# A pair's first product copied into the bank of its second summand, and T4 in place of B22, in a block chain of fp32 layers on one core

## The chip, the core and the metric

The kernel runs on one core of a Trainium2 chip. The metric is the device time of one execution in microseconds (us), median of several runs. A NeuronCore has five engines with a queue of instructions each: PE (TensorE, matrix products), ACT (ScalarE), DVE (VectorE), POOL (GpSimd) and SP (SyncE, which here only issues transfers). They run side by side and wait for each other by semaphores only. Sixteen DMA engines carry out what SP, POOL and ACT issue. TensorE reads SBUF and writes PSUM, which has 8 banks of 128 x 512 fp32.

## The reference

The input is 256 tokens of 1024 features. The program is a chain: a convolution module, an FFN, a gated injection (PLE), a differential attention block, a second FFN, a second PLE, and a second block with ten input projections. What the change touches are the two FFNs, with d_ff = 2816:

```
def swiglu(x, w_gate, w_up, w_down):
    return (jax.nn.silu(x @ w_gate) * (x @ w_up)) @ w_down
...
u = rms_norm(h, ffn_norm_g[i])
h = h + swiglu(u, ffn_w_gate[i], ffn_w_up[i], ffn_w_down[i])
```

## The kernel before

**Pieces.** All weights are cut into pieces of 128 x 2048 fp32 (1 MB). Each piece is an operation o in one fixed order (STREAM, FFN_ORDER, lines 54 to 72). SP loads pieces in that order into a ring of four buffers (`raw`, line 337); a buffer is free when the low part of its old piece has been made. For precision each piece is split in two: ScalarE rounds it to `w_hi` (high part, line 1191), VectorE subtracts to get `w_lo` (low part, line 1737). Both have three slots, so ScalarE runs at most three pieces ahead of PE. `ahead(o)` makes the parts up to piece o+2. PE multiplies high by high, low by high, high by low.

**FFN.** The 11 chunks of 256 hidden columns (gate and up, 512 output columns) go by STEPS: chunks 0, 1 and 10 alone (`single`), and the pairs (2,3), (4,5), (6,7), (8,9) by `pair`. A pair is a 2x2 block product: two token tiles, two halves of the contraction, two chunks. It takes seven products instead of eight, by Strassen's method in Winograd's form. The left sums are made once in a layer by POOL (`first_sums`: `q_f32`, then `q_hi` by ScalarE at line 1278 and `q_lo` by POOL at 1106). The right sums are T1 = B11+B12, T2 = T1+B22 (VectorE, line 1853), T3 = T2+B21, T4 = B12+B22; they live in the three slots of `sums`: T1 in 0, T2 and then T3 in 1, T4 in 2. T1, T3 and T4 are made by POOL's transfers, one that loads and one that adds into SBUF while it moves (`accum_op`; T3 only adds to T2). T4's two transfers are issued a pair ahead, when the old T4's low part is made (lines 1127 to 1129). B22 is loaded twice, once into the ring for its own product and once inside T4.

**Order of a pair on PE** (line 578): B11, transposes of a finished chunk, T1, T2, transposes, B22, down piece, B21, T4, down piece, T3. Banks before: B11, then T2, T4 and T3 in b1; T1, then B22 in b4; B21 in bank 2; b1 and b4 change places from pair to pair. Bank 3 holds transposes, banks 4 to 7 the down product's sums.

**Order on ScalarE** (line 1286), a strict queue: high part o+2; silu of the last quarter of the pair before; copy of the first product to c_11 (1295); high part o+3 (B22); z_hi (1247); copy c_22 (1299); high part o+4; z_hi; copy c_12 (1304); high parts o+5 and o+6 (T4); silu of a quarter; o+7, o+8; two silus (1255); o+9, o+10.

**Order on VectorE** (line 1877): low part o+2; gate of the last quarter of the pair before (1838); z_lo (1831); low parts o+3, o+4; z_lo; c_12 (1892); o+5; a gate; o+6, o+7; c_11 (1900); c_22 (1903); a gate; o+8; a gate; o+9; T2 of the next pair; o+10.

POOL's order in between is `first_sums` and `weight_sums` (lines 1090 to 1130). Before these, in layer 0, POOL issues the write `toep` to DRAM at line 1055 and later two loads from it.

Of the kernel before, what the change touches and what calls it, by code (L numbers as in the profile page):

```python
# [31 lines left out]
RAW, SPLIT = 4, 3  # L32
# [52 lines left out]
SUM_SLOT = {"T1": 0, "T2": 1, "T3": 1, "T4": 2}  # L85
# [36 lines left out]
def build(nc, ws, x_tok, p_feat, par, rows, lam_rows, rel, onehot, sgu_w, pool_m, toep, u_scr, out):  # L122
    ctx = ExitStack()
    with ctx:
# [68 lines left out]
        c_11, c_22, c_12 = view(2048, 512), view(2560, 512), view(3072, 512)  # L193
# [79 lines left out]
        def operand(o):  # L273

            if o in SUM_OF_OP:
                return sums[:, SUM_SLOT[SUM_OF_OP[o][2]], :]
            return raw[:, PIECE_OF[o] % RAW, :]

        def loaded(eng, p):

            eng.wait_ge(raw_loaded[p % RAW], 16 * (p // RAW + 1))

        def operand_there(eng, o):

            if o in SUM_OF_OP:
                layer, p, name = SUM_OF_OP[o]
                sum_there(eng, layer, p, name)
            else:
                loaded(eng, PIECE_OF[o])

        def sum_there(eng, layer, p, name):

            n = pair_no(layer, p)
            if name == "T1":
                eng.wait_ge(S("t1_in"), 32 * n)
            elif name == "T4":
                eng.wait_ge(S("t4_in"), 32 * n)
# [19 lines left out]
        def _(sp):  # L317
# [5 lines left out]
            for g in range(1, NPIECE):  # L323
# [13 lines left out]
                sp.dma_start(raw[:, g % RAW, :], ws[g]).then_inc(raw_loaded[g % RAW], 16)  # L337
# [14 lines left out]
        def _(pe):  # L352
# [167 lines left out]
            def ffn(layer, m):  # L520
# [44 lines left out]
                def single(i):  # L565

                    token_chunk(("gu", layer, i), ffn_at(layer, "gu", i, 0), x_hi, x_lo,
                                ready=ready_from(m) if i == 0 else None, at={0: (0, 1), 1: (0, 2), GU - 1: (1, 2)}[i],
# [9 lines left out]
                def pair(p):  # L578
# [16 lines left out]
                    product(("p2", n), ffn_at(layer, p, "B21"), *of_x(1, t0), b2, True, (S("c_11"), 2 * n))  # L595
# [378 lines left out]
        def _(pool):  # L974
# [66 lines left out]

            def biased(n_):
# [36 lines left out]
            def second_part(name, layer, p):  # L1079

                n = pair_no(layer, p)
                if name == "T1":
                    pool.wait_ge(S("t1_in"), 32 * n - 16)
                    pool.dma_start(sums[:, 0, :], ws[B12_ROW[layer, p]], accum_op=ALU.add).then_inc(S("t1_in"), 16)
                else:
                    pool.wait_ge(S("t4_in"), 32 * n - 16)
                    pool.dma_start(sums[:, 2, :], ws[PIECE_OF[ffn_at(layer, p, "B22")]], accum_op=ALU.add) \
                        .then_inc(S("t4_in"), 16)

            def first_sums(m):  # L1090

                layer, p = PAIRED.index(m), PAIRS[0]
                pool.dma_start(sums[:, 0, :], ws[PIECE_OF[ffn_at(layer, p, "B11")]]).then_inc(S("t1_in"), 16)
# [16 lines left out]
                pool.dma_start(sums[:, 2, :], ws[B12_ROW[layer, p]]).then_inc(S("t4_in"), 16)  # L1110
                second_part("T4", layer, p)
# [7 lines left out]
            def weight_sums(layer):  # L1119

                for before, p in zip(PAIRS, PAIRS[1:]):
                    lo_ready(pool, ffn_at(layer, before, "T1"))
                    sum_there(pool, layer, before, "T2")
                    pool.dma_start(sums[:, 0, :], ws[PIECE_OF[ffn_at(layer, p, "B11")]]).then_inc(S("t1_in"), 16)
                    third_sum(layer, before)
                    second_part("T1", layer, p)
                    lo_ready(pool, ffn_at(layer, before, "T4"))
                    pool.dma_start(sums[:, 2, :], ws[B12_ROW[layer, p]]).then_inc(S("t4_in"), 16)
                    second_part("T4", layer, p)
                third_sum(layer, PAIRS[-1])  # L1130
# [12 lines left out]
            for n_ in range(2):  # L1143
# [3 lines left out]
                pool.tensor_tensor(st2[:, c], st2[:, c], st2[:, 56:57].to_broadcast([P, 8]), ALU.pow).then_inc(S("o_r"), 1)  # L1147
            pool.wait_ge(S("h_done"), 16)
# [32 lines left out]
        def _(act):  # L1181
# [59 lines left out]
            def ffn(layer, m, gname):  # L1241
# [44 lines left out]
                def pair(p):  # L1286
# [8 lines left out]
                    act.activation(c_11, bank[:, :], ACT.Copy).then_inc(S("c_11"), 1)  # L1295
# [15 lines left out]
                    act.wait_ge(S("c_11"), 2 * n)  # L1311
                    gated(one, 0, c_11[:, 0:256])
# [407 lines left out]
        def _(dve):  # L1720
# [102 lines left out]
            def ffn(layer, m, gname):  # L1823
# [19 lines left out]
                def second_sum(p):  # L1843
# [7 lines left out]
                    g = PIECE_OF[ffn_at(layer, p, "B22")]  # L1851
                    loaded(dve, g)
# [667 lines left out]
```

## Time and profile before

| | us |
|---|---|
| median of 3 runs (lowest, highest) | 1044.75 (1043.84, 1048.94) |
| the profiled execution's own time | 1044.09 |
| its span in the trace | 1042.3 |
| PE busy | 1004.0 |
| VectorE busy | 726.8 |
| ScalarE busy | 579.1 |
| first products of the pairs of layer 0, start | 132.56 |
| first products of the pairs of layer 1, start | 470.19 |

The span is shorter than the execution's time by 1.8 us, which lie before the first and behind the last instruction of the trace. The profile's weights and sums carry the name `arena` where they lie in the big scratch tensor (`sums` does), `raw` where they are in the ring. Busy time of matmuls is modelled at their ends. In rows in order of time, the brackets give the idle time before an instruction and what ended it.

### The profile page before, as it was taken

To read this page: it belongs to the slowest core of one execution; us is meant where nothing else is said; L and a number is where in the kernel's file an instruction comes from. 1 tells how busy PE (TensorE), PEld (TensorE's weight loads), DVE (VectorE), ACT (ScalarE), POOL (GpSimd) and SP (SyncE) were. 2 spreads that over 40 slices of the span, in tenths; PEclk is the share of its full clock that TensorE was granted. 3 is DMA by queue.
4 is the path that set the end of the run, shared out by engine and by line. 5 is a ranking of instruction groups with operands and counts; after the bars stand their busy time and mean duration, and the time that the engine had idled before them with its cause. 6 is when DMAs were issued, how large, how long until landed. Compare 5 with 4: busy or idle time off the path is not lost.

```text
span 1042.3 us, 13575 instructions
## 1 busy us (share of the span) xinstructions
PE 1004.0 (96%) x5398; PEld 846.7 (81%) x5398; DVE 726.8 (70%) x866; ACT 579.1 (56%) x697; POOL 168.4 (16%) x140
## 2 busy tenths in 40 slices
PE   9999959999999999998999999999999999999997
PEld 8967847877888888786778788788888888999886
DVE  6986649778757776767888766776454557777554
ACT  6427536666556677655666647654545454344433
POOL 4982530010020310171110002100000000000000
PEclk9999989999999999999999999999999999999999
DMA  8866889999554533579999854556555445554531
GB/s 322 267 189 119 308 223 319 318 302 333 216 173 150 202 133 110 187 262 258 341 331 328 253 203 160 217 194 230 186 189 202 155 169 191 177 199 162 202 121 41
DMA packets 35422, 225.23 MB, mean 216 GB/s; under 512 B 4248, under 2 KB 6808, under 8 KB 9504
## 3 DMA queue, kind: packets, MB, share of 16 engines
q1 hardware_dynamic: 24480, 171.45, 44.5%
q0 software_dynamic: 7856, 49.73, 19.1%
q10 hardware_dynamic: 3024, 3.18, 1.2%
q8 instruction: 43, 0.70, 0.3%
q14 instruction: 19, 0.16, 0.0%
HBM read 221.14 MB, written 3.21 MB: 215 GB/s over the span
## 4 chain that ended last, share of the span: by engine, by line
PE 77%; DVE 7%; DMA 5%; issue 5%; POOL 4%; ACT 1%; POOLq 0%; DVEq 0%; ACTq 0%
PE bank L393 48%; PE bank L515 10%; PE bank L484 4%; DVE w_lo L1737 4%; DMA toep<-bias_row 3%; PE bank L381 3%; PE bank L379 3%; PE bank L380 3%; DMA arena<-in_ws 2%; PE bank L429 2%; DVE arena L1853 2%; DVE arena L1838 1%; POOL w_lo L1010 1%; POOL arena L1102 1%; POOL arena L1101 1%
## 5 line engine op out<-in xcount | busy, mean ns | idle before, releaser
L1737 DVE TENSOR_TENSOR w_lo<-raw,w_hi 128x2048 fp32r<-128x2048 f32 x149 | 346.1, 2326 | 151.6 <-ACT w_hi L1191 151.1
L1191 ACT ACTIVATE w_hi<-raw 128x2048 fp32r<-128x2048 f32 x160 | 305.8, 1913 | 135.1 <-PE bank L393 115.9
L393 PE MATMUL bank<-w_hi,x_hi 128*128 128x512 f32 x544 | 149.5, 397 | 0.2
L393 PE MATMUL bank<-w_lo,x_hi 128*128 128x512 f32 x544 | 145.7, 390 | 0.0
L393 PE MATMUL bank<-w_hi,x_lo 128*128 128x512 f32 x544 | 145.7, 389 | 0.0
L393 PEld LDWEIGHTS bank<-w_hi,x_lo 128*128 128x128 f32 x544 | 102.1, 188 | 21.8
L393 PEld LDWEIGHTS bank<-w_lo,x_hi 128*128 128x128 f32 x544 | 102.1, 188 | 21.4
L393 PEld LDWEIGHTS bank<-w_hi,x_hi 128*128 128x128 f32 x544 | 98.9, 188 | 21.1 <-issue 1.8
L393 PE MATMUL bank<-w_hi,z_hi 128*128 128x512 f32 x320 | 94.2, 394 | 0.1
L393 PE MATMUL bank<-w_lo,z_hi 128*128 128x512 f32 x320 | 93.0, 390 | 0.2
L393 PE MATMUL bank<-w_hi,z_lo 128*128 128x512 f32 x320 | 92.8, 390 | 0.0
L1191 ACT ACTIVATE w_hi<-arena 128x2048 fp32r<-128x2048 f32 x32 | 61.6, 1926 | 54.9 <-DMA arena<-in_ws 19.8
L1737 DVE TENSOR_TENSOR w_lo<-arena,w_hi 128x2048 fp32r<-128x2048 f32 x32 | 72.6, 2284 | 20.0 <-ACT w_hi L1191 20.0
L381 PE MATMUL bank<-x_hi,w_lo 128*128 128x256 f32 x256 | 72.4, 283 | 0.0
L380 PE MATMUL bank<-x_lo,w_hi 128*128 128x256 f32 x256 | 72.4, 283 | 0.0
L379 PE MATMUL bank<-x_hi,w_hi 128*128 128x256 f32 x256 | 72.4, 283 | 0.0
L393 PEld LDWEIGHTS bank<-w_lo,z_hi 128*128 128x128 f32 x320 | 59.9, 188 | 13.5 <-DVE w_lo L1737 1.0
L393 PEld LDWEIGHTS bank<-w_hi,z_lo 128*128 128x128 f32 x320 | 60.1, 188 | 12.7
L1010 POOL TENSOR_TENSOR w_lo<-raw,w_hi 128x2048 fp32r<-128x2048 f32 x11 | 50.7, 4615 | 115.8 <-ACT w_hi L1191 105.3
L393 PEld LDWEIGHTS bank<-w_hi,z_hi 128*128 128x128 f32 x320 | 58.9, 188 | 12.0 <-issue 0.6
L1173 POOL TENSOR_SCALAR st<-st 128x1 f32<-128x1 f32 x2 | 0.5, 225 | 301.8 <-ACT arena L1232 301.8
L379 PEld LDWEIGHTS bank<-x_hi,w_hi 128*128 128x128 f32 x256 | 49.1, 192 | 0.0
(282 smaller groups left out, 1475.7 us busy)
## 6 DMA issues: line engine op xcount, KB each, us to landing
raw<-in_ws SPq DMA_DIRECT2D x160, 1024.0 KB, 4.9
arena<-in_ws POOLq DMA_DIRECT2D x40, 1024.0 KB, 10.8
arena<-u_scr ACTq DMA_DIRECT2D x16, 142.0 KB, 4.8
arena<-in_rows POOLq DMA_DIRECT2D x2, 1024.0 KB, 5.3
toep<-bias_row POOLq DMA_DIRECT2D x1, 1536.0 KB, 34.7
h<-in_x_tok SPq DMA_DIRECT2D x2, 512.0 KB, 4.2
raw<-in_ws SPq DMA_DIRECT2D x2, 512.0 KB, 7.7
arena<-in_rows POOLq DMA_DIRECT2D x2, 512.0 KB, 4.8
```

The source lines that it names most:

```text
L379: pe.matmul(dst, s_hi, m_hi, start=first, stop=False)
L380: pe.matmul(dst, s_hi, m_lo, start=False, stop=False)
L381: return pe.matmul(dst, s_lo, m_hi, start=False, stop=last)
L393: ins = pe.matmul(dst, tok(a_part, k, t), w_part[:, s, c], start=first and j == 0 and i == 0, stop=last and j == 2 and i == len(ks) - 1)
L429: ins = pe.transpose(banks[b][:, k * P:(k + 1) * P], src[:, k * P:(k + 1) * P], ident[:, :])
L484: ins = pe.matmul(banks[b][:, c * SEQ:(c + 1) * SEQ], w_part[:, g % SPLIT, w], x_part[:, k, :], start=j == 0 and k == 0, stop=j == 2 and k ...
L515: ins = pe.matmul(banks[b][:, :], a_part[:, k, :], w_part[:, o % SPLIT, k * 512:(k + 1) * 512], start=start and j == 0 and k == 0, stop=j ...
L1010: pool.tensor_tensor(w_lo[:, g % SPLIT, :], operand(g), w_hi[:, g % SPLIT, :].bitcast(F32), ALU.subtract).then_inc(S("lo_pool"), 1)
L1101: link(pool.tensor_tensor(q_f32[:, 2, :, :], q_f32[:, 1, :, :], a12, ALU.add))
L1191: act.activation(w_hi[:, g % SPLIT, :], operand(g), ACT.Copy).then_inc(hi_done, 1)
L1737: dve.tensor_tensor(w_lo[:, g % SPLIT, :], operand(g), w_hi[:, g % SPLIT, :].bitcast(F32), ALU.subtract).then_inc(lo_done, 1)
L1853: dve.tensor_tensor(sums[:, 1, :], sums[:, 0, :], raw[:, g % RAW, :], ALU.add).then_inc(S("t2"), 1)
```

## The change

It has four parts. (1) The three banks of a pair rotate from pair to pair (`pair_banks`), and ScalarE copies the first product not to SBUF but into the bank b2, where B21's product is then accumulated onto it; VectorE's sum c_11 is gone, and both engines read the bank. (2) B22 is loaded once, into slot 2 of `sums`, outside the ring, by SP (a layer's first by POOL); when its low part and T2 are made, POOL adds B12 onto it, which gives T4. (3) T3's transfer is issued behind T4's. (4) A layer's first T1 is loaded and summed earlier. The single chunks' banks change accordingly.

```
+SUM_SLOT = {"T1": 0, "T2": 1, "T3": 1, "T4": 2, "B22": 2}
+RINGS = [o for o in PIECES if o not in B22_OF_OP]
+def pair_banks(p):
+    return [(1 + PAIRS.index(p) + j) % 3 for j in range(3)]
...
@@ SP
+            for o in PIECES[1:]:
+                if o in B22_OF_OP:
+                    layer, p, _ = B22_OF_OP[o]
+                    if p != PAIRS[0]:
+                        lo_ready(sp, ffn_at(layer, PAIRS[PAIRS.index(p) - 1], "T4"))
+                        sp.dma_start(sums[:, 2, :], ws[PIECE_OF[o]]).then_inc(S("b22_in"), 16)
+                    continue
+                g = RING_OF[o]
                 if g >= RAW:
-                    old = PIECES[g - RAW]
-                    lo_ready(sp, old)
-                    for layer in range(2):
-                        for p in PAIRS:
-                            if old == ffn_at(layer, p, "B22"):
-                                sum_there(sp, layer, p, "T2")
+                    lo_ready(sp, RINGS[g - RAW])
...
@@ PE
-                    b1, b2 = n % 2, 2
-                    b4 = 1 - b1
+                    b1, b4, b2 = pair_banks(p)
-                    product(("p1", n), ffn_at(layer, p, "B11"), *of_x(0, t0), b1, True, (S("c_11"), 2 * n - 1))
+                    product(("p1", n), ffn_at(layer, p, "B11"), *of_x(0, t0), b1, True, (S("c_11"), n))
...
-                    product(("p2", n), ffn_at(layer, p, "B21"), *of_x(1, t0), b2, True, (S("c_11"), 2 * n))
+                    released[b2] = (S("c_11"), n)
+                    product(("p2", n), ffn_at(layer, p, "B21"), *of_x(1, t0), b2, False, (S("hidden"), MADE_NO[layer, one, 0]))
...
@@ POOL
+            def second_part(name, layer, p):
+                ...
+                else:
+                    lo_ready(pool, ffn_at(layer, p, "B22"))
+                    sum_there(pool, layer, p, "T2")
+                    pool.dma_start(sums[:, 2, :], ws[B12_ROW[layer, p]], accum_op=ALU.add).then_inc(S("t4_in"), 16)
+            def first_part(layer):
+                p = PAIRS[0]
+                pool.dma_start(sums[:, 0, :], ws[PIECE_OF[ffn_at(layer, p, "B11")]]).then_inc(S("t1_in"), 16)
...
             pool.wait_ge(S("v_split"), len(BLOCKS))
+            first_part(0)
             biased(1)
+            second_part("T1", 0, PAIRS[0])
             pool.wait_ge(S("h_done"), 4)
...
@@ POOL, first_sums
-                pool.dma_start(sums[:, 0, :], ws[PIECE_OF[ffn_at(layer, p, "B11")]]).then_inc(S("t1_in"), 16)
...
-                second_part("T1", layer, p)
-                pool.wait_ge(S("q_hi"), layer + 1)
                 pool.wait_ge(S("q_sums"), layer + 1)
-                pool.tensor_tensor(flat4(q_lo), flat4(q_f32), flat4(q_hi).bitcast(F32), ALU.subtract).then_inc(S("q_lo"), 1)
                 for n_ in range(2):
                     for t in range(TT):
                         pool.wait_ge(*jobs[(m, n_, t)])
-                pool.dma_start(sums[:, 2, :], ws[B12_ROW[layer, p]]).then_inc(S("t4_in"), 16)
-                second_part("T4", layer, p)
+                pool.dma_start(sums[:, 2, :], ws[PIECE_OF[ffn_at(layer, p, "B22")]]).then_inc(S("b22_first"), 16)
+                pool.wait_ge(S("q_hi"), layer + 1)
+                pool.tensor_tensor(flat4(q_lo), flat4(q_f32), flat4(q_hi).bitcast(F32), ALU.subtract).then_inc(S("q_lo"), 1)
...
@@ POOL, weight_sums
+                for p, after in zip(PAIRS, PAIRS[1:] + [None]):
+                    if after:
+                        lo_ready(pool, ffn_at(layer, p, "T1"))
+                        sum_there(pool, layer, p, "T2")
+                        pool.dma_start(sums[:, 0, :], ws[PIECE_OF[ffn_at(layer, after, "B11")]]).then_inc(S("t1_in"), 16)
+                    second_part("T4", layer, p)
+                    third_sum(layer, p)
+                    if after:
+                        second_part("T1", layer, after)
...
@@ POOL, between attention and the wait for its end
+            first_part(1)
+            second_part("T1", 1, PAIRS[0])
             pool.wait_ge(S("h_done"), 16)
...
@@ ScalarE
-                    act.activation(c_11, bank[:, :], ACT.Copy).then_inc(S("c_11"), 1)
+                    k = PAIRS.index(p)
+                    act.wait_ge(S("hidden"), MADE_NO[layer, PAIRS[k - 1][0] if k else 1, 1])
+                    act.activation(banks[pair_banks(p)[2]][:, :], bank[:, :], ACT.Copy).then_inc(S("c_11"), 1)
...
-                    act.wait_ge(S("c_11"), 2 * n)
-                    gated(one, 0, c_11[:, 0:256])
+                    bank, _ = take(act, ("p2", n))
+                    gated(one, 0, bank[:, 0:256])
...
@@ VectorE
-                    g = PIECE_OF[ffn_at(layer, p, "B22")]
-                    loaded(dve, g)
-                    dve.tensor_tensor(sums[:, 1, :], sums[:, 0, :], raw[:, g % RAW, :], ALU.add).then_inc(S("t2"), 1)
+                    sum_there(dve, layer, p, "B22")
+                    dve.tensor_tensor(sums[:, 1, :], sums[:, 0, :], sums[:, 2, :], ALU.add).then_inc(S("t2"), 1)
...
-                    dve.wait_ge(S("c_11"), 2 * n - 1)
-                    dve.tensor_tensor(c_11, p_2[:, :], c_11, ALU.add).then_inc(S("c_11"), 1)
...
-                    gated(one, 0, c_11[:, 256:512])
+                    gated(one, 0, p_2[:, 256:512])
```

## Rows read from the trace of the kernel before

**Rows 1.** The page's first part: busy us, share of the span, instructions.
```profile
PE 1004.0 (96%) x5398; PEld 846.7 (81%) x5398; DVE 726.8 (70%) x866; ACT 579.1 (56%) x697; POOL 168.4 (16%) x140
```

**Rows 2.** Waits of PE: who waited for whom, us in total, times, longest.
```profile
PE bank L515 <- DVE arena L1838: 10.5, 6, 1.8
```

**Rows 3.** PE in order of time: start, us, op, [idle before <-releaser].
```profile
147.03 1.09 PE L530 MATMUL bank<-ident,arena 128*128 128x128 f32 x4 [11.59 <-DVE arena L1838]
...
182.78 1.16 PE L515 MATMUL bank<-w_hi,q_hi 128*128 128x512 f32 x4 [1.75 <-DVE arena L1838]
...
477.38 0.74 PE L530 MATMUL bank<-ident,arena 128*128 128x128 f32 x4 [4.31 <-DVE arena L1838]
```

**Rows 4.** ScalarE in order of time, same columns.
```profile
142.25 1.91 ACT L1191 ACTIVATE w_hi<-arena 128x2048 fp32r<-128x2048 f32 x1 [13.52 <-DMA arena<-in_ws]
...
213.47 0.60 ACT L1295 ACTIVATE arena<-bank 128x512 f32<-128x512 f32 x1 [0.39 <-PE bank L515]
...
472.60 1.91 ACT L1191 ACTIVATE w_hi<-arena 128x2048 fp32r<-128x2048 f32 x1 [6.25 <-DMA arena<-in_ws]
```

**Rows 5.** Busy us of each engine by stretch, granted clock, DMA share, GB/s.
```profile
140.00:150.00 10.00, 2.97 (x9) 2.52 (x10) 5.27 (x4) 3.13 (x4) 0.86 (x1) 0.51 0.69 184
215.61:248.45 32.84, 31.10 (x140) 25.60 (x141) 27.04 (x19) 21.28 (x19) 3.14 (x5) 1.00 1.02 319
```

**Rows 6.** VectorE in order of time, columns as for PE.
```profile
235.42 0.69 DVE L1903 TENSOR_TENSOR arena<-arena,bank 128x512 f32<-128x512 f32 x1 [0.54 <-PE bank L515]
...
241.23 2.28 DVE L1853 TENSOR_TENSOR arena<-arena,raw 128x2048 f32<-128x2048 f32 x1
...
247.83 0.47 DVE L1838 SCALAR_TENSOR_TENSOR arena<-bank,st,arena 128x256 f32<-128x256 f32 x1
...
465.91 5.01 DVE L1737 TENSOR_TENSOR w_lo<-raw,w_hi 128x2048 fp32r<-128x2048 f32 x1 [4.53 <-ACT w_hi L1191]
```

**Rows 7.** Chain that ended last, in order of time: start, us, what.
```profile
121.11 3.40 POOL arena L1102
...
164.27 5.45 PE bank L515 x24
...
262.80 5.44 PE bank L515 x24
268.24 5.44 PE bank L393 x24
...
458.74 3.33 POOL arena L1102
...
494.61 5.45 PE bank L515 x24
```

**Rows 8.** DMA, 215.61 to 248.45: SP's queue, packets, MB, engines' share.
```profile
q1 hardware_dynamic: 720, 5.24, 38.7%
```

**Rows 9.** Issue L1087 (T4's accumulate, eight times): us to landing.
```profile
DMA to landing us min/median/max: 7.9/9.4/11.8
```

**Rows 10.** DMA, 149 to 151: POOL's queue alone.
```profile
q0 software_dynamic: 53, 0.43, 104.2%
```

**Rows 11.** Issue L1116 (T3's accumulate) at 215.4: us to landing.
```profile
DMA to landing us min/median/max: 15.2/15.2/15.2
```

**Rows 12.** Issue L1084 (T1's accumulate) at 223.5: us to landing.
```profile
DMA to landing us min/median/max: 14.5/14.5/14.5
```

**Rows 13.** DMA, 163 to 170: both queues.
```profile
q0 software_dynamic: 143, 1.04, 66.2%
q1 hardware_dynamic: 133, 0.96, 33.8%
```

**Rows 14.** Issue L1110 (plain load to slot 2, twice): us to landing.
```profile
DMA to landing us min/median/max: 6.9/7.3/7.7
```

**Rows 15.** The page's DMA issues: KB each, us to landing; issued at 75.59.
```profile
toep<-bias_row POOLq DMA_DIRECT2D x1, 1536.0 KB, 34.7
```

**Rows 16.** Issue L1093 (B11's load to slot 0) at 114.0: us to landing.
```profile
DMA to landing us min/median/max: 17.6/17.6/17.6
```

More of the change, by code:

```diff
@@ L84 @@
 B12_ROW = {(layer, p): NPIECE + NPAIR * layer + i for layer in range(2) for i, p in enumerate(PAIRS)}
-SUM_SLOT = {"T1": 0, "T2": 1, "T3": 1, "T4": 2}
+SUM_SLOT = {"T1": 0, "T2": 1, "T3": 1, "T4": 2, "B22": 2}
+B22_OF_OP = {ffn_at(layer, p, "B22"): (layer, p, "B22") for layer in range(2) for p in PAIRS}
+RINGS = [o for o in PIECES if o not in B22_OF_OP]
+RING_OF = {o: r for r, o in enumerate(RINGS)}
+def pair_banks(p):
+    return [(1 + PAIRS.index(p) + j) % 3 for j in range(3)]
 def pair_no(layer, p):
@@ L192, in build @@
         hids = [view(1536, 2, 256), view(3584, 2, 256), view(11264, 2, 256)]
-        c_11, c_22, c_12 = view(2048, 512), view(2560, 512), view(3072, 512)
+        c_22, c_12 = view(2560, 512), view(3072, 512)
         sums = view(5120, 3, HALF)
@@ L276, in operand, with loaded @@
                 return sums[:, SUM_SLOT[SUM_OF_OP[o][2]], :]
-            return raw[:, PIECE_OF[o] % RAW, :]
-        def loaded(eng, p):
-            eng.wait_ge(raw_loaded[p % RAW], 16 * (p // RAW + 1))
+            if o in B22_OF_OP:
+                return sums[:, SUM_SLOT["B22"], :]
+            return raw[:, RING_OF[o] % RAW, :]
+        def loaded(eng, o):
+            r = RING_OF[o]
+            eng.wait_ge(raw_loaded[r % RAW], 16 * (r // RAW + 1))
         def operand_there(eng, o):
@@ L287, in operand_there @@
                 sum_there(eng, layer, p, name)
+            elif o in B22_OF_OP:
+                sum_there(eng, *B22_OF_OP[o])
             else:
-                loaded(eng, PIECE_OF[o])
+                loaded(eng, o)
         def sum_there(eng, layer, p, name):
@@ L295, in sum_there @@
                 eng.wait_ge(S("t1_in"), 32 * n)
+            elif name == "B22":
+                if p == PAIRS[0]:
+                    eng.wait_ge(S("b22_first"), 16 * (layer + 1))
+                else:
+                    eng.wait_ge(S("b22_in"), 16 * (n - layer - 1))
             elif name == "T4":
-                eng.wait_ge(S("t4_in"), 32 * n)
+                eng.wait_ge(S("t4_in"), 16 * n)
             elif name == "T2":
@@ L322, in _ @@
             sp.dma_start(raw[:, 0, D:HALF], ws[0][:, D:HALF]).then_inc(raw_loaded[0], 16)
-            for g in range(1, NPIECE):
+            for o in PIECES[1:]:
+                if o in B22_OF_OP:
+                    layer, p, _ = B22_OF_OP[o]
[4 more added lines that the diff above has]
+                g = RING_OF[o]
                 if g == RAW:
@@ L567, in single @@
                     token_chunk(("gu", layer, i), ffn_at(layer, "gu", i, 0), x_hi, x_lo,
-                                ready=ready_from(m) if i == 0 else None, at={0: (0, 1), 1: (0, 2), GU - 1: (1, 2)}[i],
+                                ready=ready_from(m) if i == 0 else None, at={0: (0, 1), 1: (2, 0), GU - 1: (2, 0)}[i],
                                 release=lambda t: (S("hidden"), MADE_NO[layer, i, t]),
@@ L1040, in _ @@
             pool.wait_ge(S("x_scaled_1"), 2)
+            def second_part(name, layer, p):
+                n = pair_no(layer, p)
+                if name == "T1":
+                    pool.wait_ge(S("t1_in"), 32 * n - 16)
+                    pool.dma_start(sums[:, 0, :], ws[B12_ROW[layer, p]], accum_op=ALU.add).then_inc(S("t1_in"), 16)
+                else:
+                    lo_ready(pool, ffn_at(layer, p, "B22"))
[4 more added lines that the diff above has]
+                pool.dma_start(sums[:, 0, :], ws[PIECE_OF[ffn_at(layer, p, "B11")]]).then_inc(S("t1_in"), 16)
             def biased(n_):
@@ L1119, in weight_sums @@
             def weight_sums(layer):
[L1121 to L1128, printed above, removed]
+                for p, after in zip(PAIRS, PAIRS[1:] + [None]):
[3 more added lines that the diff above has]
+                        pool.dma_start(sums[:, 0, :], ws[PIECE_OF[ffn_at(layer, after, "B11")]]).then_inc(S("t1_in"), 16)
                     second_part("T4", layer, p)
-                third_sum(layer, PAIRS[-1])
+                    third_sum(layer, p)
+                    if after:
+                        second_part("T1", layer, after)
             h_factor(0)
@@ L1903, in pair @@
                     dve.tensor_tensor(c_22, c_22, u_3[:, :], ALU.subtract).then_inc(S("c_22"), 1)
-                    dve.wait_ge(S("c_11"), 2 * n)
-                    gated(one, 0, c_11[:, 256:512])
+                    gated(one, 0, p_2[:, 256:512])
                     ahead(o + 6)
```

11 lines of the change are left out of this document (1 added, 10 removed).

## The prediction, made before the changed kernel was run

> **What bounds the kernel now.** I began with the busy shares: PE 96% [rows 1]. Such an engine can gain only where it stands still, so next I read who PE waits for. Nearly all of it is in the two FFN stages: 15.9 us in two waits at L530 and 10.5 us in six at L515, all released by L1838, VectorE's gated product [rows 2]. PE's order of time tells the two kinds apart.
>
> The two at L530 (11.6 us in layer 0, 4.3 us in layer 1 [rows 3]) are in front of a layer's first pair. L1838 itself was late there because ScalarE stood before T1's high part, 13.52 and 6.25 us, until the transfer had landed [rows 4]. In that stretch the granted clock is 0.51 of full speed, so 1.2 GHz for much of it, after PE had stood still [rows 5].
>
> The six at L515, 1.75 us each, are T1's product in the later pairs [rows 3]: its bank is the one that the pair before used for its last quarter, and VectorE frees it only at 247.83+0.47 [rows 6]. A pair lasts 32.84 us; PE is busy 31.10 of it, and the 16 DMA engines are full (share 1.02) [rows 5]. Without stalls PE would need 7 products and 2 down pieces, 7x2.72+2x5.44, and 0.36 for a group of transposes twice: 30.7 us (2.72 is half of a two-product row of 5.45; 5.44 is a down row, as at 268.24 [rows 7]).
>
> **The banks and the removed sum.** The rotation gives T1 a bank that was freed long before: 6x1.75 = 10.5 us at most. The wait doesn't vanish. ScalarE's copy of the first product now goes into the bank of that same last quarter and waits for the same VectorE product. Behind it on ScalarE stand B22's high part, z_hi and the copy c_22; VectorE's z_lo and low part of B22 wait for those. VectorE's sum c_11 goes, of the size of c_22's 0.69, but VectorE was idle 0.54 before the next sum, waiting for PE [rows 6]: alone it is worth nothing, below nothing it can't be. The copy itself, PSUM to PSUM, has no row. The one PSUM to SBUF takes 0.60 [rows 4]; bounds half of it and twice, 0.3 and 1.2, taken 0.6. The gates then read a bank instead of SBUF, as the last quarter's gate already does: nothing.
>
> **T4 in place of B22.** Before, slot 2 got B12 and then B22 by two POOL transfers, one pair ahead; B22 was also loaded to the ring. Now B22 is loaded once and B12 is added after B22's low part is made and T2 is summed. This takes one plain MB of ten out of each pair. Plain loads cost 38.7% of 32.84 us for 5.24 MB, 2.4 us each [rows 8]; so DMA falls from 33.6 us (1.02 of 32.84) to about 31.2 per pair. But T4 now cannot start before VectorE finishes B22's low part, and PE has only B22, down and B21 (2.72+5.44+2.72 = 10.9 us) before it wants T4. An accumulating MB from issue to landing: 7.9 least, 9.4 median, 11.8 most [rows 9]. I take the 7.9, at 145.00: there only that queue moved data, as I expect at the new place, since SP's five loads fall due behind T4's low part and need 12 to 14 us. The high part adds 1.9 us, and the silu, the gate and VectorE's low part queue behind it.
>
> So there is a closed ring, pair by pair (start to start on each engine: a high part 1.85, a low part 2.2, a gate 0.4, c_22 0.6). From T4's landing: high part 1.9, silu and gate 0.9, low parts of T4 and down 4.4, c_22 and gate 1.0, T3 low and gate 2.6, B11 low 2.2 = 13.0. Then T2 sum and two low parts 6.6, last gate 0.5 = 7.1 (235.42 to 241.23 and to 248.30 are the same steps before [rows 6]). Then copy 0.5, B22 high 1.85, z_hi 0.6, z_lo 0.7, B22 low 2.3 = 6.0. Issue to landing 8.0. Sum 34.1 us, against 32.9 now ((262.80-164.27)/3 [rows 7]).
>
> Two more things must have landed by 13.0 us or the ring lengthens: next T1 and next B22. On POOL's queue T3 and T1 follow T4 (POOL now issues T3 behind B22's low part). Alone an accumulating MB takes about 5 us of all engines (0.43 MB in 2 us at share 1.04 [rows 10]; I take 5.2). Beside SP's loads it takes 7.4: T3 landed at 215.4+15.2 = 230.6 [rows 11] and T1 behind it at 223.5+14.5 = 238.0 [rows 12], and both queues then move as much, 1.04 and 0.96 MB in 7 us [rows 13]. SP issues next B22 when T4's low part ends, at 4.9, and bytes flow from 6.9; T1 (from 5.2; alone to 6.9, beside SP's after it) lands at 12.2 to 12.6, B22 near 13.0. That is level with VectorE. I put 0.5 us on each period: 34.6. Bounds: 34.1 (none late) and 37.4 (T4 9.4, T3 and T1 7.4 each, then the 7.1+6.0 and 0.1 back to B22's low part). The other ring pieces wait behind that B22 on SP, but have 10 us and more.
>
> **Layer starts.** Layer 1: T1 is summed near 430, long before need. POOL's four sums end as before (458.74+3.33 = 462.1 [rows 7], less 0.6 for the load moved away), B22's load is issued, 6.9 to 7.7 us as L1110's [rows 14]: landed by 469. PE now waits for VectorE: B11's low part ran 465.91 to 470.9, 5.01 us instead of 2.29 [rows 6]. Then z_lo, T1's low part and two gates to 474.2, T2's sum 476.4, high part 478.3; then copy, B22 high, z, B22 low to 484.1, T4 landed 492.0. T4's product ends 5.9 later (high 1.9, silu and gate 0.9, low 2.2, the last four matmuls 0.9), 497.9, where it ended at 494.61+5.45 less 0.2 of pipeline = 499.9 [rows 7]: gain 2.0.
>
> Layer 0: the first half's load is issued behind the toep write on POOL's queue, which lands at 110.3 (75.59+34.7 [rows 15]). POOL waits for that load, to about 113.5 instead of 110.9, so its sums end at 127.3 instead of 121.11+3.40 = 124.5 [rows 7], and B11's low part again overlaps POOL's q_lo: PE loses 1.6 us at B11. B22's first load lands behind T1's accumulate and both toep loads: 131.6 for the old B11 load (114.0+17.6 [rows 16]), plus 2.6, plus 7.4 = 141.6, say 142. T2's sum then ends at 144.3 instead of 149.5; T4's product ends at 165.8 instead of 169.5: gain 3.7. If the queue lets it past (bound 139.8, when VectorE is ready) 5.9; if it lands at 146, nothing.
>
> On that low part of 5.01 us: the Trainium skill (SBUF — State Buffer, "Who interferes with whom") says that a VectorE instruction with two SBUF inputs contends with a GpSimd one that reads SBUF. The trace agrees, 5.01 against 2.29 us while L1106 ran. Without it layer 0's loss at B11 would be nothing, and T2 there would still wait for B22.
>
> **Sum.** -2.0 -3.7 +6x(34.6-32.9) = +4.5 us. Six is three periods in each layer. The profiled execution took 1044.09 us (span 1042.3), 0.7 below the median of 1044.75. 1044.1+4.5 = 1048.6: no measurable change, at the upper edge of it; 0.5%, 5.2 us, is about what a measurement of this kernel can tell from none.
>
> **Rivals.**
> - *Slower: the transfers set the ring.* From 34.7 us per period it is over 0.5%. At 36 us (T4 landing in 9.3 us, or T1 and B22 1.9 us late) it is -5.7+18.6 = +12.9, 1057; at 37.4 with both first T4s 1.5 late +24, 1068. For: the median accumulate is 9.4 us [rows 9]. Against: one MB less, and the burst falls at another time. The Trainium skill (DMA: Bandwidth & Descriptors, "Queues, rings and completion order") has each DMA engine go round robin between queues by packets, so T1 would be stretched just when SP's burst comes. The trace agrees: equal bytes in 163 to 170 [rows 13].
> - *Faster: T4 is in time.* Were it landed 2 us sooner than any row shows, or were ScalarE's and VectorE's work ordered with more slack than I count, only ScalarE's copy would be late, some 0.5 us a pair: 31.2 per period, -5.7-10.2 = -16, 1028. For: PE's stall is real and its bank is free. Against: no accumulate landed under 7.9. Half of it, 33 us, gives 1039.
> - *Layer 0 gives nothing*, as B22 queues behind toep until 146 or later: +8, 1052; counted with the slower ones.
>
> **How the numbers follow.** Forecast 0.44, slower 0.42, faster 0.14. The forecast's own range is 1040 to 1049. For 8 in 10: down to 1038 (period 32.9, starts as computed), up to 1061 (period 36.5, which also holds a copy of 1.2 us). Above 1061 and below 1038 I leave about 0.1 each. So 0.14 faster, 0.44 same, 0.42 slower.
>
> **What would show it.** PE's waits at L515 for L1838 gone or small; in their place PE waits inside each pair at T4's product, 1 to 4 us, released by VectorE's low part, and ScalarE waits for a transfer to slot 2 five to eight us eight times; a pair 34 to 35 us long; DMA share per pair below 0.95; L530's wait under 5 us in layer 0 and about 1.5 in layer 1; clock no longer halved in front of layer 1's first pair. Wrong if ScalarE never waits for T4, or if VectorE stands before T2's sum for a transfer by more than 1 us.

## The result, and the profile after

| | before | after |
|---|---|---|
| median, us (lowest, highest) | 1045.1 (1043.84, 1048.94) | 1055.84 (1054.33, 1059.57) |
| ratio, 95% interval | | 1.0114 (1.0093 to 1.0135) |
| profiled execution, us (span) | 1044.09 (1042.3) | 1059.57 (1057.8) |
| DMA, MB | 225.23 | 216.83 |

The changed kernel is 10.7 us slower: inside the range of 1038 to 1061, but slower, where no measurable change was forecast. (The kernel before ran once more beside it; 1044.75 was the median of the first three.) The profiled execution was the longest of four (the other spans: 1052.5, 1053.9, 1054.1), so single terms read from it come out some 4 us too large in sum.

The page's first part [rows 1]: PE's share is the same 96%, with 13 us more of it for the same 5398 instructions. A matmul's end is modelled, and the first group of four behind a wait has 1.20 us where one in the flow has 1.07; some groups behind a long wait took 2 us, at a lower granted clock. So a busier PE is here a PE that waits more often. How the 13 us divide between the two is not shown.

```profile
PE 1017.2 (96%) x5398; PEld 844.1 (80%) x5398; DVE 724.2 (68%) x858; ACT 576.1 (54%) x697; POOL 163.3 (15%) x134
```

The waits of the kernel after (who waited for whom, us in total, times, longest). L536 is L515 of before, L551 is L530, L1217 and L1765 are the high and low part, L1323 the copy into the bank, L1866 the gate, L1880 the sum T2, L1072 T4's accumulate.

```profile
ACT w_hi L1217 <- DMA arena<-in_ws: 58.7, 14, 7.9
ACT bank L1323 <- DVE arena L1866: 15.3, 6, 2.6
PE bank L536 <- DVE w_lo L1765: 10.2, 11, 1.3
PE bank L536 <- ACT w_hi L1217: 9.0, 8, 2.1
PE bank L536 <- ACT bank L1323: 3.3, 4, 1.5
PE bank L551 <- DVE arena L1866: 3.3, 2, 2.1
DVE arena L1880 <- DMA arena<-in_ws: 0.9, 2, 0.7
```

PE's waits for the gate at L515 [rows 2] are gone, and L530's 15.9 us are 3.3. In their place are 22.5 us in small waits in the pairs, most of them for the high and the low part of T4. The last row is the test that the prediction named as making it wrong, and it did not.

The chain that ended last, two stretches of it: from T2's low part over the last gate to the copy, and a pair later from B22's high part to T4's product (start, us, what). This is the ring of the prediction, read from the trace (the row of 9.57 us is T4's accumulate, from its issue to its landing):

```profile
211.94 2.38 DVE w_lo L1765 x2
...
216.26 0.49 DVE arena L1866
...
216.84 0.04 ACT bank L1323
...
252.28 1.91 ACT w_hi L1217
254.19 0.49 ACT z_hi L1273
...
254.78 0.69 DVE z_lo L1859
255.47 2.21 DVE w_lo L1765
257.68 0.36 issue
258.04 9.57 DMA arena<-in_ws
...
270.04 0.49 DVE arena L1866
270.53 2.21 DVE w_lo L1765
272.74 0.04 issue
272.79 1.21 PE bank L536 x4
```

ScalarE in order of time: its wait for T4, the wait for T3 (237.09), the copy behind the gate, the next wait for T4 [rows 4].

```profile
231.27 1.91 ACT L1217 ACTIVATE w_hi<-arena 128x2048 fp32r<-128x2048 f32 x1 [6.47 <-DMA arena<-in_ws]
...
237.09 1.93 ACT L1217 ACTIVATE w_hi<-arena 128x2048 fp32r<-128x2048 f32 x1 [1.71 <-DMA arena<-in_ws]
...
251.79 0.58 ACT L1323 ACTIVATE bank<-bank 128x512 f32<-128x512 f32 x1 [2.58 <-DVE arena L1866]
...
267.63 1.91 ACT L1217 ACTIVATE w_hi<-arena 128x2048 fp32r<-128x2048 f32 x1 [7.89 <-DMA arena<-in_ws]
```

PE in order of time at T4's product, the first and the last of layer 0 and the first of layer 1 [rows 3]. Starts of these four products in layer 0: 163.51, 197.82, 233.23, 269.59; in layer 1: 502.54, 539.93, 574.36, 609.35.

```profile
163.51 1.20 PE L536 MATMUL bank<-w_hi,q_hi 128*128 128x512 f32 x4 [0.38 <-ACT w_hi L1217]
...
269.59 1.20 PE L536 MATMUL bank<-w_hi,q_hi 128*128 128x512 f32 x4 [2.12 <-ACT w_hi L1217]
...
502.54 1.20 PE L536 MATMUL bank<-w_hi,q_hi 128*128 128x512 f32 x4 [1.99 <-ACT w_hi L1217]
505.74 2.08 PE L536 MATMUL bank<-w_lo,q_hi 128*128 128x512 f32 x4 [0.70 <-DVE w_lo L1765]
```

A period, here and below, is the time from T4's product in one pair to T4's product in the next. The stretches from one T4 product's end to the next, to 0.2 us (window, length, busy us of PE, PEld, DVE, ACT and POOL, granted clock, DMA share, GB/s) [rows 5]. The DMA engines are no longer full (0.82 to 0.91 where the share was 1.02 [rows 5]), and yet the pair is longer. That no engine is short of time and the pair grows all the same is what a chain of waits would do; the experiments test it.

```profile
167.80:202.00 34.20, 32.48 (x141) 24.97 (x140) 26.06 (x19) 20.80 (x19) 3.15 (x4) 1.00 0.91 277
202.00:237.40 35.40, 32.63 (x141) 25.05 (x140) 26.24 (x19) 19.93 (x19) 3.14 (x4) 1.00 0.88 268
237.40:273.80 36.40, 32.63 (x141) 25.07 (x141) 26.30 (x19) 20.47 (x18) 1.75 (x2) 1.00 0.82 257
507.80:544.10 36.30, 33.29 (x141) 26.13 (x140) 25.35 (x19) 20.41 (x17) 3.20 (x4) 0.96 0.83 253
544.10:578.50 34.40, 32.59 (x141) 25.01 (x141) 26.14 (x19) 20.30 (x19) 3.18 (x4) 1.00 0.86 267
578.50:613.60 35.10, 32.69 (x143) 25.12 (x142) 26.28 (x19) 19.68 (x18) 1.76 (x2) 1.00 0.83 259
```

### The profile page after: what moved, and what is told of

It is laid out like the page before. It is cut to its first block, busy times and chain, and to the rows that moved or that the text cites. A ratio compares the mean times of both kernels' runs of the same rounds, so it can differ in the third digit from the quotient of the medians.

```text
span 1057.8 us, 13549 instructions
## 1 busy us (share of the span) xinstructions
PE 1017.2 (96%) x5398; PEld 844.1 (80%) x5398; DVE 724.2 (68%) x858; ACT 576.1 (54%) x697; POOL 163.3 (15%) x134
## 2 busy tenths in 40 slices
DMA packets 34269, 216.83 MB, mean 205 GB/s; under 512 B 4120, under 2 KB 6680, under 8 KB 9376
## 3 DMA queue, kind: packets, MB, share of 16 engines
q0 software_dynamic: 6992, 43.44, 17.8%
## 4 chain that ended last, share of the span: by engine, by line
PE 69%; DVE 15%; issue 7%; ACT 4%; DMA 3%; POOL 2%; DVEq 0%; POOLq 0%; ACTq 0%
PE bank L414 50%; DVE w_lo L1765 7%; PE bank L536 5%; DVE bank L2038 4%; PE bank L402 3%; PE bank L400 3%; PE bank L401 3%; DMA arena<-in_ws 3%; PE bank L450 2%; ACT w_hi L1217 1%; DVE arena L1880 1%; DVE arena L1866 1%; DVE z_lo L1859 1%; PE bank L643 1%; PE bank L804 0%
## 5 line engine op out<-in xcount | busy, mean ns | idle before, releaser
L1765 DVE TENSOR_TENSOR w_lo<-raw,w_hi 128x2048 fp32r<-128x2048 f32 x141 | 332.4, 2363 | 128.7 <-ACT w_hi L1217 122.3
L1217 ACT ACTIVATE w_hi<-raw 128x2048 fp32r<-128x2048 f32 x152 | 290.7, 1913 | 108.6 <-PE bank L414 86.3
L1217 ACT ACTIVATE w_hi<-arena 128x2048 fp32r<-128x2048 f32 x40 | 76.7, 1918 | 102.6 <-DMA arena<-in_ws 58.7
L1765 DVE TENSOR_TENSOR w_lo<-arena,w_hi 128x2048 fp32r<-128x2048 f32 x40 | 90.9, 2283 | 5.3 <-ACT w_hi L1217 5.3
L536 PE MATMUL bank<-w_hi,q_hi 128*128 128x512 f32 x128 | 38.3, 422 | 12.5 <-ACT w_hi L1217 9.0
```

Source lines behind the costliest of these rows:

```text
L536: ins = pe.matmul(banks[b][:, :], a_part[:, k, :], w_part[:, o % SPLIT, k * 512:(k + 1) * 512], start=start and j == 0 and k == 0, stop=j ...
L1217: act.activation(w_hi[:, g % SPLIT, :], operand(g), ACT.Copy).then_inc(hi_done, 1)
L1765: dve.tensor_tensor(w_lo[:, g % SPLIT, :], operand(g), w_hi[:, g % SPLIT, :].bitcast(F32), ALU.subtract).then_inc(lo_done, 1)
```

## The experiments

The theory: a closed ring runs through T4's accumulate (T4 landed, its parts, VectorE's work up to T2, last gate, copy, B22's parts, accumulate issued), and it is longer than PE's work of a pair. Rivals: the banks and ScalarE's copy cost the time; the early T1 does, through POOL; or the lost time is DMA contention.

**The three parts by themselves.** e1 has only part 1:

```
+def pair_banks(p):
+    return [(1 + PAIRS.index(p) + j) % 3 for j in range(3)]
-                    act.activation(c_11, bank[:, :], ACT.Copy)...
+                    act.wait_ge(S("hidden"), MADE_NO[layer, PAIRS[k - 1][0] if k else 1, 1])
+                    act.activation(banks[pair_banks(p)[2]][:, :], bank[:, :], ACT.Copy)...
```

> Only part 1 of the change: the rotating banks and ScalarE's copy into the bank of B21's product; B22 in the ring and both of T4's transfers as before. Theory (T4's late accumulate closes a ring of waits and is the whole loss): PE's 1.75 us wait at T1 goes, nothing takes its place but about 0.5 us at B22; a pair shortens from 32.9 to 31.4-32.5 us, the latter if the DMA engines' 33.6 us of work per pair hold it; 1036 to 1043 us. Rival (the copy that waits for the gate is the loss): a pair lasts 34 us or more and the kernel is slower than before, 1050 or more.

Measured: 1036.11 us, ratio 0.9909 (0.9891 to 0.9928). The periods of layer 0 are 31.48, 31.48 and 31.50 (T4's products at 167.22, 198.70, 230.18, 261.68), those of layer 1 are 32.1, 31.5 and 31.9. A window of one, columns as above:

```profile
198.70:230.18 31.48, 31.42 (x141) 25.35 (x140) 26.26 (x19) 20.89 (x18) 3.69 (x5) 1.00 1.02 329
```

PE is busy in all of it but 0.06. ScalarE's copy waits 2.5 us for the gate in this kernel too (six times, 15.3 us), and PE waits for the copy 0.4 us in all. The banks are worth 8.9 of the 10.5 us of PE's stall, and the copy's wait costs next to nothing while T4 is there a pair ahead.

e2 has only parts 2 and 3: the changed kernel with the hunks of part 1 and of the early T1 taken back. (Part 3, T3's transfer behind T4's, has no run of its own.)

> Only parts 2 and 3: B22 once in slot 2, B12 added onto it, T3 behind it; banks, c_11 and the layers' starts as before. Theory: the ring of waits is closed by T4 alone, only T1's product in front of it now also waits for the last gate; a pair lasts 34 to 35.5 us, ScalarE waits 5 to 8 us for slot 2 eight times, total +8 to +18 us, 1053 to 1063. Rival (the copy is the loss): within 3 us of before.

Measured: 1056.15 us, ratio 1.0102 (1.0082 to 1.0123). The sum was met, the way to it was not: three of the six periods are 32.9, as before, held by the old bank wait (PE for the gate: 14.0 us, six times), and three are 37.5, 36.0 and 37.2. As I read it, the ring is shorter here, because B22's high part does not stand behind a copy that waits for the gate. Where T4 was late, the bank wait grew to 2.90 and the matmul groups behind it were slow:

```profile
186.23 2.04 PE L536 MATMUL bank<-w_hi,q_hi 128*128 128x512 f32 x4 [2.90 <-DVE arena L1862]
188.07 1.74 PE L536 MATMUL bank<-w_hi,q_lo 128*128 128x512 f32 x4
189.65 1.08 PE L536 MATMUL bank<-w_lo,q_hi 128*128 128x512 f32 x4
190.57 1.07 PE L536 MATMUL bank<-w_hi,q_hi 128*128 128x512 f32 x4
```

That product took 4.3 us instead of 2.7. The granted clock of the whole stretch was 0.95. The two make (2.90-1.75)+(4.3-2.7) = 2.7 of the 4.6 us by which that period (37.5) is longer. Another 1.5 is the T4 product with which it begins: its parts came late, so it took 4.2 us (167.21 to 171.43) instead of 2.7. Some 0.4 stay unexplained.

e3 has only part 4, the layer's first T1 loaded and summed early (`first_part` and `second_part` ahead of the stage; T4 and banks as before).

> Only part 4: a layer's first T1 loaded and summed early. Theory: layer 1 gains most of its 4.3 us wait and the lower clock behind it (3 to 6 us), layer 0 gains less, since POOL stands for the first half behind the toep write and so makes h_factor late, which VectorE waits for: 3 to 7 us of the 11.6; in all 5 to 12 us faster, 1033 to 1040. Rival (the early transfer only moves the wait): within 2 us of before.

Measured: 1039.17 us, ratio 0.9945 (0.9926 to 0.9964). PE's wait at L530 is 3.3 us in two, where it was 15.9, but 3.1 us come back as VectorE's wait for POOL (below). More is lost in the pairs: four of the six periods are 32.9 as before, one in each layer is longer, 35.6 and 35.1. In that of layer 0 ScalarE stood 2.73 and 2.84 us for transfers into `sums`, and T1's bank came 2.84 us late for PE instead of 1.75. The cause in layer 1 is not shown.

```profile
202.18 1.93 ACT L1198 ACTIVATE w_hi<-arena 128x2048 fp32r<-128x2048 f32 x1 [2.84 <-DMA arena<-in_ws]
...
209.66 1.17 PE L515 MATMUL bank<-w_hi,q_hi 128*128 128x512 f32 x4 [2.84 <-DVE arena L1845]
```

e4 has parts 1 and 4 without T4 in place, and POOL's second T1 transfer of layer 0 behind `h_factor(0)`:

```
             biased(1)
-            second_part("T1", 0, PAIRS[0])
...
             h_factor(0)
+            second_part("T1", 0, PAIRS[0])
             first_sums(0)
```

> Parts 1 and 4 without T4 in place, and in layer 0 POOL waits for the first half only behind h_factor(0). Theory: the gains of the two parts add up, and VectorE no longer stands for h_factor; 1024 to 1036. Rival (the DMA engines' 10 MB per pair, 33.6 us of work, hold the pair at 32.8 whatever the waits): 1036 to 1040.

Measured: 1029.34 us (1028.6 to 1031.03), ratio 0.9848 (0.9828 to 0.9867). It beats both kernels. Its periods are 33.5, 31.8 and 31.6 in layer 0, and 31.5, 31.8 and 31.5 in layer 1; the second, with DMA as full as before:

```profile
193.25:225.03 31.78, 31.71 (x142) 25.30 (x140) 26.36 (x19) 20.89 (x18) 3.67 (x5) 1.00 1.02 329
```

In the first, of 33.5 us, DMA is as full (1.02), but there a load was late: VectorE stood 1.91 us for B22 in the ring before T2's sum, and PE 1.73 us for the copy behind it.

```profile
170.52 2.29 DVE L1867 TENSOR_TENSOR arena<-arena,raw 128x2048 f32<-128x2048 f32 x1 [1.91 <-DMA raw<-in_ws]
...
178.43 1.17 PE L520 MATMUL bank<-w_hi,q_hi 128*128 128x512 f32 x4 [1.73 <-ACT bank L1309]
```

So the parts alone give -8.9, +11.2 and -5.8 us against before, -3.5 in sum, and together they gave +10.7. Parts 1 and 4 take away stalls of PE. My reading is that once the ring sets the time, a stall less on PE is only a longer wait for T4; e4 against e8 (below) bears it out for the sum, and no run does for each part.

**The accumulate in the ring.** e5 leaves B12 out of T4: the transfer onto slot 2 is not there, and T4's parts are made of B22 once T2 is summed (`wait_ge(S("t2"), n)`).

```
-                    pool.dma_start(sums[:, 2, :], ws[B12_ROW[layer, p]], accum_op=ALU.add).then_inc(S("t4_in"), 16)
```

> The changed kernel without the transfer that adds B12 onto B22: slot 2 keeps B22 and T4's product is computed from it (so its output lacks B12 in T4); everything else, the banks, the copy and the order of the queues, is the changed kernel's. Theory (the ring through T4's accumulate): ScalarE no longer waits at T4, a pair lasts 31.0 to 31.8 us instead of 34.3 to 36.4; about 8 x 3 = 20 to 27 us faster than the changed kernel, 1029 to 1036. Rival (the copy's wait, or SP's later load of B22, holds the pair): 33.5 us or more, above 1045.

Measured: 1027.7 us, ratio 0.9837 (0.982 to 0.9854), 28 us less than the changed kernel, and 1.3 us under the lowest that I had expected. Periods are 31.47, all six.

```profile
193.50:224.90 31.40, 31.35 (x141) 25.30 (x140) 26.19 (x19) 20.89 (x18) 2.26 (x3) 1.00 0.83 268
```

e6 has that transfer, but as a plain load over B22 (T4 is then B12 alone):

```
-                    pool.dma_start(sums[:, 2, :], ws[B12_ROW[layer, p]], accum_op=ALU.add).then_inc(S("t4_in"), 16)
+                    pool.dma_start(sums[:, 2, :], ws[B12_ROW[layer, p]]).then_inc(S("t4_in"), 16)
```

> The changed kernel with the transfer of B12 as a plain load over B22 instead of one that adds (T4 is then B12 alone). Same place, same wait, half of the engines' work. Theory: it lands about 5 to 5.5 us after its issue instead of 7.9 to 9.6, which is 2.5 to 4 us earlier; the pair's ring shortens by that, to 31.2-32 us: 1032 to 1040. Rival (a fixed latency of the queue, not the adding, makes it late): it lands after 7 us or more and the time stays above 1047.

Measured: 1039.06 us, ratio 0.9944 (0.9925 to 0.9963). This load's time from issue to landing (eight times):

```profile
DMA to landing us min/median/max: 5.7/6.1/6.3
```

and one of its periods, which run from 32.4 to 33.5 where I had expected 31.2 to 32:

```profile
197.08:230.56 33.48, 32.25 (x142) 25.12 (x140) 26.43 (x19) 21.06 (x19) 2.88 (x4) 1.00 0.87 284
```

The period can be added up: with 6.1 us in place of the accumulate the ring's other terms, as the changed kernel's trace has them on average (13.2, 7.4, 5.9, and 0.3 before the issue, see the table below), make 32.9; the mean of the six is 33.0.

The same place in the program with no transfer, with one of 6.1 us and with one of 8.4 us: 1027.7, 1039.1, 1055.8. From the second to the third, 8 landings of some 2.5 us more (mean 8.6 against about 6.1) make 20 us; 17 were measured. From none to the second, 11. So the time follows this one landing, while DMA stands at 0.83, 0.87 and 0.88 in these three. Full DMA engines as the cause of the whole fall with it. (The eight do occupy the engines longer when they accumulate: POOL's queue has 17.8% of the changed kernel's span and 16.4% of e6's, for the same 43.44 MB. That is 188 against 170 us, 2.3 us for each.)

The same reading in the changed kernel (L1072, eight times):

```profile
DMA to landing us min/median/max: 7.9/8.4/9.6
```

Pair by pair it was 7.9, 7.9, 8.2, 9.6 in layer 0 and 9.5, 9.2, 8.0, 8.6 in layer 1. Two of these, the 9.6 and the 8.6, have SP's loads beside them, the last pairs of each layer, where no next B22 holds SP's queue back. Of 223.0 to 231.2, then of 258.0 to 267.6, by queue (packets, MB, share of the 16 engines):

```profile
q0 software_dynamic: 172, 1.28, 84.0%
...
q0 software_dynamic: 175, 1.30, 73.6%
q1 hardware_dynamic: 55, 0.45, 12.5%
```

**Is it T3's transfer, issued 0.55 us behind T4's, that stretches T4's?** e9 lets POOL wait:

```
                 lo_ready(pool, ffn_at(layer, p, "T2"))
+                pool.wait_ge(S("t4_in"), 16 * pair_no(layer, p))
                 pool.dma_start(sums[:, 1, :], ...
```

> The changed kernel with one wait more on POOL: T3's transfer is issued only when T4's has landed (T1's second half, behind it on the queue, is later too). Open is why T4's accumulate took 7.9 us in some pairs and 9.2 to 9.6 in others. Theory A, T3's packets stretch T4's, since both are issued 0.55 us apart: then alone all eight land in 7.9 us or less, with the smallest near 7.3. Theory B, the spread comes from elsewhere (SP's loads beside two of them, or the accumulate itself): minimum stays at 7.8 to 7.9 and the largest stays above 9. Either way T3 now lands about 8.3 us behind T4 (0.5 of issue, 2.6 before bytes move, 5.2 of bytes) where it was 5.8, and ScalarE wants it 4.2 behind T4: I expect ScalarE's wait before T3's high part to grow from 1.7 to about 4 us and the period by 1 to 3 us, so 1062 to 1074 in all. If the time falls, the sharing between T4's and T3's transfers was worth more than T3's delay.

Measured: 1076.55 us, ratio 1.0306 (1.026 to 1.0353), more than the 1074 that I gave as the upper end. T4's landings, now without T3 in flight:

```profile
DMA to landing us min/median/max: 7.9/8.4/9.8
```

They are the same, so theory A falls. The time went where it was expected: ScalarE's waits for transfers into `sums` are 107.9 us (58.7 in the changed kernel), the copy was 2.2 us late for PE in each later pair, and a pair took 38 to 39 us. What makes the 9.5 and 9.2 us of layer 1, with POOL's queue moving data and SP's none, stays open.

**Two mends of the changed kernel.** e7 puts the silu of (two, 0) ahead of T4's high part on ScalarE:

```
-                    ahead(o + 4)
                     act.wait_ge(S("c_12"), 2 * n)
                     gated(two, 0, c_12[:, 0:256])
+                    ahead(o + 4)
```

> The changed kernel with one swap on ScalarE: the silu of the pair's second chunk, first tile, ahead of T4's high part instead of behind it. Theory: VectorE makes its gate while T4 is still under way, so its low part of T4 starts 0.9 us sooner after the landing; six periods and two last pairs shorter by 0.9 each, -5 to -7 us against the changed kernel: 1049 to 1051. Rival (the end is set by the transfers of T1 and B22, not by VectorE's queue): less than 2 us.

Measured: 1052.36 us, ratio 1.0078 (1.0058 to 1.0098): 3.5 us less than the changed kernel, of 5 to 7. By the medians, taking 0.9 us of ScalarE and VectorE off the ring gave some 0.4 us a pair. Its six periods are 34.6, 34.6, 36.0, 33.5, 34.4 and 34.1, but in its fastest execution of four, where the changed kernel's trace is its slowest. ScalarE now stands 1.2 us for T3 in the first two pairs, where it was 0.8: part of the gain goes into the next transfer of the ring.

e8 is the changed kernel with e4's move of POOL's transfer.

> The changed kernel with layer 0's second transfer of T1 behind h_factor(0) on POOL, instead of in front of the wait for the end of the convolution. Theory: POOL's wait for the first half (until 117.36 in the profile) made h_factor late, VectorE stood 6.07 us and PE 1.78 us at the lower clock; without it the first pair starts 3 to 3.7 us sooner and the whole kernel is 2 to 4 us faster than the changed one: 1052 to 1054. Rival (B22's first load, behind toep's, sets T2 in layer 0 anyway): no change, 1056.

Measured: 1052.98 us, ratio 1.0083 (1.0062 to 1.0104), so 2.9 us less. In the changed kernel POOL waits for the first half of T1 and only then makes h_factor(0), for which VectorE stands:

```profile
117.36 0.92 POOL L1068 DMA_DIRECT2D arena<-in_ws  x1 [21.57 <-DMA arena<-in_ws]
...
120.73 0.72 POOL L1113 TENSOR_TENSOR st<-st 128x2 f32<-128x2 f32 x1
...
121.49 3.39 DVE L1765 TENSOR_TENSOR w_lo<-raw,w_hi 128x2048 fp32r<-128x2048 f32 x1 [6.07 <-POOL st L1113]
```

With the transfer behind it, h_factor is done at 113.8 and T4's first product starts at 160.53 instead of 163.51: the 3.0 us arrive whole. e4 and e8 have the same early T1 and the same banks; between them lie parts 2 and 3 alone, T4 in place with T3 behind it: +23.6 us.

e10 has both mends.

> The changed kernel with both mends at once: layer 0's second T1 transfer behind h_factor(0) (alone -2.9 us) and the silu of (two, 0) ahead of T4's high part (alone -3.5 us). The ring theory has them add, since one acts ahead of the first pair and the other inside each period: 1055.8 - 6.4 = 1049.4, range 1047.5 to 1051. If they don't add (1052 to 1053), the layer start was only hidden by the same wait for T4. Either way it stays slower than the kernel before and 20 us over the kernel with the banks and the early T1 alone (1029.3).

Measured: 1052.18 us (8 runs, 1050.46 to 1057.44), ratio 1.0073 (1.0051 to 1.0096). They don't add: 1049.4 over 1044.7 would be a ratio of 1.0045, and lies outside. Its first T4 product starts at 160.27, against 160.53 of e8; its periods are 34.9, 34.7, 36.8 and 36.1, 33.8, 34.3, so the silu's move gives nothing on top here. The landings of T4 explain little of it: the six periods without them come to 161.4 us in the changed kernel, 158.0 in e7, 159.7 in e8 and 159.1 in e10, so the move took 3.4 us off the one kernel and 0.6 off the other. Why, stays open; the runs of one of these kernels lie 3 to 7 us apart.

## Why the prediction was right in kind and too low

**The ring: right, its last term too short.** From T4's landing (231.2) to its next (267.6) are 36.4 us in this pair, the longest of layer 0; term by term, predicted, measured there, and the mean of the six periods:

| term | predicted | measured | mean of six |
|---|---|---|---|
| landing to T2's sum | 13.0 | 13.4 (231.2 to 244.6) | 13.2 |
| T2's sum, two low parts, last gate | 7.1 | 7.1 (to 251.7) | 7.4 |
| copy to B22's low part | 6.0 | 6.0 (to 257.7) | 5.9 |
| T4's accumulate with its issue | 8.0 | 9.9 (to 267.6) | 9.0 |
| sum | 34.1 | 36.4 | 35.5 |

The 0.4 in the first row is T3, whose transfer the prediction did not ask about: it was wanted 4.2 us behind T4, came 5.8 behind it, ScalarE stood 1.71 us and VectorE's gate 0.24 us more. T1 and B22, on which the prediction put its 0.5 us, were late for VectorE twice in eight pairs, 0.9 us in all. The 7.4 has one pair in it, the second of layer 1, where the T4 product before it was late and slow and VectorE then stood 1.3 us for ScalarE; the other five have 7.2. The term that was mis-sized is the accumulate: 1.0 of the 1.4 us by which the mean exceeds 34.1, where the prediction had put 0.5 on top, and for other transfers. I took the smallest row, 7.9 of 7.9/9.4/11.8 [rows 9], on the ground that only POOL's queue would move data. That held in six pairs, and in two of those it took over 9 us all the same; in the last pair of a layer SP's ring loads were beside it. The mean landing was 8.6. The Trainium skill (DMA: Bandwidth & Descriptors, "Queues, rings and completion order") has an engine take turns between the queues that have work; the last pair of layer 0 agrees, 9.6 us with SP's 0.45 MB beside it against 8.2 us in the pair before. The other two show that this is not all.

In the profiled execution the six periods came to 34.3, 35.4, 36.4, 37.4, 34.4 and 35.0, 212.9 in all, where 6x34.6 = 207.6 was forecast and 197.1 was before: +15.8 instead of +10.2. (The forecast took 32.9 for the old period; its own row gives 98.53/3 = 32.84, which is 0.3 us in six.) The first of layer 1 holds 0.8 us of the T4 product that it begins with, whose last group ran at the lower clock (2.08 instead of 1.20, at 505.74); counted from product end to product end it is 36.5, and the six are 212.1.

**Layer 0's start: half right.** T4's product ended at 167.7, 1.8 us sooner than before, where 3.7 was predicted. The prediction had POOL wait to 113.5; it waited to 117.36, since the load landed 3.9 us behind the time that I drew from the toep write. What it did not see is who stands behind POOL there: h_factor(0), and VectorE for it (6.07 us), so PE's first B11 product started 3.7 us later than before (136.24 against 132.56). e8 takes just this out, and 3.0 us come back. B22 landed at 143.2 (142 predicted), T2's sum ended at 145.5 (144.3), VectorE's low part beside POOL's took 5.04 us (as [rows 6]).

**Layer 1's start: wrong in sign.** It begins 6.3 us behind from layer 0 (VectorE's B11 low part at 472.18, 465.91 before). From there T2's sum ended at 483.0 (482.7 predicted with that offset) and B22's low part at 490.7 (490.4). Then the accumulate landed at 500.6 instead of 498.3, and the product ended 7.0 us behind it instead of 5.9, PE having stood 1.99 us and then run slow. So 507.6 instead of 504.2: +1.4 us where -2.0 was forecast. Again the accumulate, and what a wait of PE costs behind itself. The clock in front of the pair was as predicted:

```profile
472.00:482.00 10.00, 8.80 (x41) 6.97 (x40) 9.82 (x6) 3.27 (x5) 3.05 (x1) 1.00 0.51 187
482.00:492.00 10.00, 8.15 (x34) 5.95 (x34) 7.43 (x5) 8.98 (x8) 1.53 (x3) 1.00 0.32 105
...
502.00:508.00 6.00, 4.76 (x13) 3.34 (x14) 4.98 (x4) 4.98 (x5) 0.00 (x0) 0.67 1.05 217
```

So it is 1.00 in front of the pair, where it was 0.83 in the kernel before in the 10 us behind L530's wait (476 to 486), and 0.67 behind the wait for T4: the lower clock did not go, it moved.

**Sum.** -5.7+10.2 = +4.5 predicted. In the profiled execution it is -1.8+1.4 for the starts, +15.0 for the periods (212.1-197.1), and 0.9 behind the last pairs: 15.5, which is its span against before's. The median execution was 10.7 slower; how it divides no trace shows. All three terms missed to the same side. The time is inside the stated range because the range's upper end took a period of 36.5; the forecast itself, no measurable change, did not come.

**The banks: right.** Up to 10.5 us, and it was 8.9 alone (e1). The copy took 0.58, 0.6 taken. That its wait enters the ring is right as well: the copy stands in the chain, behind the gate. In e2, without that copy, three periods stayed at 32.9; since the old bank wait is back there too, this alone does not prove it.

**The rivals.** "T4 is in time", 31.2 per period and 1028, was priced right: without the accumulate it is 31.47 and 1027.7 (e5). "The transfers set the ring" was the nearest to what happened, through T4's landing and T3's, and not through B22's. "From 34.7 us per period" was the point from which it decides, and 34.6 lay 0.1 under it: that closeness was seen, and the chances of 0.44 and 0.42 say it. What did not lean the right way is the choice of the least row for a term that each pair passes through.

**What was to be seen.** PE's waits at T4's product were 1.5 to 3 us (two waits, high and low part), ScalarE's 6.2 to 8.3 us, the DMA share 0.82 to 0.91, L530's 2.09 and 1.20: as listed. The pair of 34 to 35 us held in three of six.

## What to carry to other kernels

A transfer that starts only when this turn's results are made, and which the same turn needs, is a link of a ring: price it with the mean of its landings at least, never with the least, and ask for each further transfer that is issued behind it (here T3's) when it is wanted. Removing bytes from full DMA engines is worth nothing if it is paid with such a link: here the second load of B22, one MB of ten in each pair, let T4 be made a pair ahead, and giving it up cost 24 us (e8 against e4). And try the parts of a change one by one: two of the four parts were worth 15.7 us together with one transfer moved on its queue, and the whole hid them.

## What the runs showed that was not expected

A 1 MB load from POOL's queue to the same slot took 5.7 to 6.3 us from issue to landing (e6) and 7.9 to 9.6 us when it accumulates, in six of eight cases with no load of SP beside it: some 2 us for the addition alone. Its spread of 1.7 to 1.9 us stays without T3's transfer behind it (e9). The spread has a place: in the first three pairs of layer 0 the landing took 7.8 to 8.2 us in all six traces with T4 in place (the changed kernel, e2, e7 to e10), while in layer 1 each of them has at least one landing of 9.0 us or more with no load of SP beside it. The cause is open.

A DMA share of 1.02 was no bound by itself: it was 1.02 at 32.84 us per pair [rows 5] and at 31.48 us (e1), with 319 and 329 GB/s, so the queued loads in part only used what time there was. Nor was it free. In e4 and e3 it stood at 1.02 and 0.99 in periods of 33.5 and 35.6 us, in which an engine stood 1.9 to 2.8 us for a late transfer. And e5, which moves two MB less in a pair (share 0.83), has six equal periods, 188.8 us in all, where e4's come to 191.6. So it delayed single loads and not every pair.
